# The output gate's units placed behind the last head pair, and the finished rows cut beside that pair's states

## The reference, cut to what matters

```python
def first_block(x, ...):
    h = rmsnorm(x) * (1 + scale) + shift
    p = h @ w_in
    c_val, c_gate, c_og, ts, r_og, g_conv, g_rwkv = split(p)
    u = causal_depthwise_conv(c_val * sigmoid(c_gate), 31 taps)
    u = silu(layernorm(u) * ln_g + ln_b) * silu(c_og)
    y_conv = u @ w_conv_out
    o = rwkv7_scan(token_shift(ts), ...)
    o = groupnorm_and_bonus(o) * silu(r_og)
    y_rwkv = o @ w_rwkv_out
    m = sigmoid(g_conv) * y_conv + sigmoid(g_rwkv) * y_rwkv
    return x + gate * (m @ w_out)
```

## Time and profile before

| | |
|---|---|
| median of 3 runs | 2361.52 us (2360.99 to 2362.99) |
| the profiled execution | 2362.81 us |
| its span in the trace | 2361.5 us, 44695 instructions |
| PE busy | 2215.4 us, 94% of the span |
| DVE, ACT, POOL busy | 1462.9, 938.0, 462.2 us (62, 40, 20%) |
| the scan's periods and all before them | 0 to 680 us |
| last pair's states to the end of stage 5 | 680 to 956 us |
| second block | 956 us to the end |

### The profile page before, as it was taken

How to read it: one execution, slowest core, us unless ns; L and a number is a source line. 1 busy time by engine, 2 the same in 40 slices (tenths; PEclk the granted TensorE clock), 3 DMA queues, 4 the chain that set the end, 5 groups by cost and what they waited for, 6 DMA issues and landing times.

```text
span 2361.5 us, 44695 instructions
## 1 busy us (share of the span) xinstructions
PE 2215.4 (94%) x19538; PEld 1947.2 (82%) x19538; DVE 1462.9 (62%) x2338; ACT 938.0 (40%) x1590; POOL 462.2 (20%) x277
## 2 busy tenths in 40 slices
PE   4898999999997999987998999999999999999999
PEld 1677777777766787976888999999988889999987
DVE  3687888888867443496556666633355556777722
ACT  1324434344332434433544444322456655444411
POOL 0344343344310344423231000000000011000000
PEclk7899999999998999997999999999999999999999
DMA  6541011111115324310013223223311013223231
GB/s 237 128 111 55 11 42 42 42 42 42 42 60 173 107 90 126 118 38 10 21 37 112 90 90 91 91 92 94 109 45 37 21 36 115 90 90 90 86 107 67
DMA packets 60290, 184.75 MB, mean 78 GB/s; under 512 B 7200, under 2 KB 11296, under 8 KB 60096
## 3 DMA queue, kind: packets, MB, share of 16 engines
q1 hardware_dynamic: 60096, 181.90, 24.9%
HBM read 174.99 MB, written 6.88 MB: 77 GB/s over the span
## 4 chain that ended last, share of the span: by engine, by line
PE 74%; DVE 16%; ACT 5%; issue 2%; DMA 1%; POOL 0%; SPq 0%; DVEq 0%; ACTq 0%
PE PS L540 59%; PE PS L670 4%; DVE ca L1874 3%; PE PS L1025 2%; PE PS L1152 1%; PE PS L865 1%; PE PS L1120 1%; DVE Swk L2273 1%; DVE mx L2269 1%; DVE kx L1942 1%; PE PS L998 1%; DVE Bf L1948 1%; DMA xt<-in_xT 1%; ACT Lb L1200 1%; DVE acc L1804 1%
## 5 line engine op out<-in xcount | busy, mean ns | idle before, releaser
L2560 POOL TENSOR_TENSOR wlo<-raw,whi 128x1024 fp32r<-128x1024 f32 (+2 forms) x154 | 310.4, 2017 | 926.5 <-ACT whi L1200 921.1
L540 PE MATMUL PS<-nhi,whi 128*128 128x264 f32 x2064 | 440.1, 294 | 12.5 <-DVE nlo L2115 6.9
L540 PE MATMUL PS<-nlo,whi 128*128 128x264 f32 x2064 | 423.1, 287 | 0.0
L540 PE MATMUL PS<-nhi,wlo 128*128 128x264 f32 x2064 | 420.4, 285 | 0.0
L1200 ACT ACTIVATE whi<-raw 128x1024 fp32r<-128x1024 f32 (+3 forms) x322 | 306.4, 953 | 226.4 <-PE PS L540 199.4
L540 PEld LDWEIGHTS PS<-nhi,whi 128*128 128x128 f32 x2064 | 324.0, 191 | 22.1 <-DVE qB L2157 5.6
L540 PEld LDWEIGHTS PS<-nlo,whi 128*128 128x128 f32 x2064 | 324.6, 190 | 0.0
L540 PEld LDWEIGHTS PS<-nhi,wlo 128*128 128x128 f32 x2064 | 324.0, 191 | 0.0
L1786 DVE TENSOR_TENSOR wlo<-raw,whi 128x1024 fp32r<-128x1024 f32 (+1 forms) x168 | 201.1, 1197 | 171.9 <-ACT whi L1200 171.6
L540 PE MATMUL PS<-hhi,whi 128*128 128x512 f32 x648 | 264.5, 408 | 7.4 <-DVE hlo L1853 7.3
L540 PE MATMUL PS<-hhi,wlo 128*128 128x512 f32 x648 | 258.4, 399 | 1.6 <-POOL wlo L2560 1.6
(11 more groups left out here) (351 smaller groups left out, 3533.8 us busy)
## 6 DMA issues: line engine op xcount, KB each, us to landing
raw<-in_wall SPq DMA_DIRECT2D x282, 512.0 KB, 3.6
raw<-in_wall SPq DMA_DIRECT2D x16, 384.0 KB, 3.1
TZ<-g_rows SPq DMA_DIRECT2D x2, 2112.0 KB, 8.4
raw<-in_wall SPq DMA_DIRECT2D x32, 128.0 KB, 2.0
raw<-in_wall SPq DMA_DIRECT2D x16, 256.0 KB, 2.6
g_rows<-gsb SPq DMA_DIRECT2D x8, 328.0 KB
xt<-in_xT SPq DMA_DIRECT2D x1, 2048.0 KB, 13.8
o_rows<-os SPq DMA_DIRECT2D x8, 256.0 KB, 2.2
```

What stands on the lines that cost most here:

```text
L540: q = e.matmul(out, cuts[a][:, k * P:(k + 1) * P], (hi_, lo_)[b][:, kr, lo:lo + w], start=start and k == 0 and a == b == 0, stop=stop and ...
L2560: e.tensor_tensor(wlo[slot[i]][:, w], raw[i % NRAW][:, w], whi[slot[i]][:, w].bitcast(F32), ALU.subtract).then_inc(*up("lo_pool", i))
```

## The change

What it does, part by part:

- **Last pass.** The ninth pass of `PERIOD` goes; the string `LAST` runs in its place. It has eleven fill units, not three: gate 6, gate 7, rog 7 and the eight units of the output gate c_og (stage 2 is gone from its old place). Between pieces of two f stands one state step of pair 7; the letter y cuts one finished row (ACT `yhi`, DVE `ylo`), k = 0 to 7. Row 7 is cut straight from `os`, without the way through DRAM. The SiLU of c_og unit p waits for the lower part of row p, since both live in `keep8[p]`.
- **Transfers.** SP loads rows 0 to 6 back once the last core step of pair 7 is done (`KV_sum`), before the last pass.
- **rwkv_out.** Its weights' remainder moves from DVE to POOL (`ON_POOL`). The ada units leave this stage. The mean's matmul comes after its sixth unit, into bank 6.
- **g_conv.** The squares of the layer norm run from the seventh rwkv_out unit to the second g_conv unit, the variance's matmul after the third g_conv unit, the normalising and SiLU after it, and the product with `keep8` and the split of its rows beside g_conv units 5 to 7.
- **conv_out.** The ada units stand between its units; their sums live in `t1b`. DVE's two instructions for each now come in the rounds of this stage.
- **out.** The one-column matmuls for `mod` come after its first unit.

```diff
-ON_POOL = ("w_in", "a_in", "out", "a_out", "b_out", "conv_out")
+ON_POOL = ("w_in", "rwkv_out", "a_in", "out", "a_out", "b_out", "conv_out")
...
+LAST = ("fft" + 6 * "sfft" + "sffy" "sfffy" "sfffyt" "sfffy" "fffyffyffy" "s" "fffy" + 35 * "ft")
...
+    if j == 8:
+        return [("gate", 6, 0), ("gate", 7, 0), ("rog", 7, 0)] + [("og", n, 0) for n in range(8)]
...
     for j in range(8):
         units.append(("rwkv_out", j * P, 0, 8))
-        units.append(("ada", 4 + j // 4, j % 4, 8))
-    for base in (2048, 7296):
-        for j in range(8):
-            units.append(("w_in", base + j * P, 0, 8))
+    for j in range(8):
+        units.append(("w_in", 7296 + j * P, 0, 8))
     for j in range(8):
         units.append(("conv_out", j * P, 0, 8))
+        units.append(("ada", 4 + j // 4, j % 4, 8))
...
-        gates = [sb("macc2", z1 + 98304, S), sb("macc3", z1 + 100352, S)]
+        gates = [t1b[:, 0, :], t1b[:, 1, :]]
...
-            for j in range(9):
-                run(PERIOD, ...)
+            for j in range(8):
+                run(PERIOD, ...)
+            run(LAST, s=side(7), f=fill(8), t=nothing(), y=nothing())
...
+                if j == 5:
+                    on.wait_ge(*at("oc", 7))
                     on.wait_ge(*at("conv_sum"))
-                    e.matmul(PS[:, 2, :], ones, acc2[:, :], start=True, stop=True).then_inc(*up("mean_sum"))
+                    e.matmul(PS[:, 6, :], ones, acc2[:, :], start=True, stop=True).then_inc(*up("mean_sum"))
...
                 full("w_in", hhi, hlo, halves(S, b))
+                if j == 2:
+                    on.wait_ge(*at("conv_sq", 7))
+                    e.matmul(PS[:, 7, :], ones, acc1[:, :], start=True, stop=True).then_inc(*up("var_sum"))
...
                 full("out", mhi, mlo, halves(S, b), (lambda k: on.wait_ge(*at("m", k))) if j == 0 else None)
+                for g in (4, 5) if j == 0 else ():
+                    on.wait_ge(*at("ada_dve", ada_unit[g, 3]))
+                    on.wait_ge(*at("mm", 7))
+                    for n in range(4):
+                        q = e.matmul(PS[:, g, n:n + 1], gates[g - 4][:, n * P:(n + 1) * P],
+                                     con[:, CONE:CONE + 1], start=True, stop=True)
...
+                    elif kind == "og":
+                        on.wait_ge(*at("y", p))
+                        act(keep8[:, p, :], src, ACT.Silu).then_inc(*up("og", p))
...
-            on.wait_ge(*at("os", 7))
-            on.wait_ge(s_od, 128)
-            for k in range(8):
-                if k % 4 == 0:
-                    on.wait_ge(s_ol[k // 4], 64)
-                act(yhi[:, k, :], keep8[:, k, :], ACT.Copy).then_inc(*up("y_hi", k))
+            def cut_rows():
+
+                for k in range(8):
+                    if k == 0:
+                        on.wait_ge(*at("Ph", 7))
+                    if k < 7:
+                        on.wait_ge(s_ol[k // 4], (64, 48)[k // 4])
+                    else:
+                        on.wait_ge(*at("os", 7))
+                    act(yhi[:, k, :], keep8[:, k, :] if k < 7 else os_[:, :], ACT.Copy).then_inc(*up("y_hi", k))
+                    yield
...
-                for k in (0, 1, 2) if j == 0 else (j + 2,) if j < 6 else ():
+                for k in {5: (0, 1, 2), 6: (3, 4), 7: (5, 6, 7)}.get(j, ()):
...
-                on.wait_ge(*at("os", j))
-                e.dma_start(odram[j * P:(j + 1) * P, :], os_[:, :]).then_inc(s_od, 16)
-            on.wait_ge(s_od, 128)
-            for k in range(8):
+                if j < 7:
+                    on.wait_ge(*at("os", j))
+                    e.dma_start(odram[j * P:(j + 1) * P, :], os_[:, :]).then_inc(s_od, 16)
+            on.wait_ge(s_od, 112)
+            on.wait_ge(*at("KV_sum", 7))
+            for k in range(7):
                 e.dma_start(keep8[:, k, :], odram[k * P:(k + 1) * P, :]).then_inc(s_ol[k // 4], 16)
```

More of the change, by code:

```diff
@@ L1378, in scalar, with squares @@
             run(BEFORE, c=nothing(), s=nothing(), p=prep(0), f=fill(-1), t=nothing())
-            for j in range(9):
-                run(PERIOD, c=core(j) if j < 8 else nothing(), s=side(j - 1) if j else nothing(),
-                    p=prep(j + 1) if j < 7 else nothing(), f=fill(j), t=nothing())
-            on.wait_ge(*at("os", 7))
-            on.wait_ge(s_od, 128)
-            for k in range(8):
-                if k % 4 == 0:
-                    on.wait_ge(s_ol[k // 4], 64)
-                act(yhi[:, k, :], keep8[:, k, :], ACT.Copy).then_inc(*up("y_hi", k))
+            def cut_rows():
[8 more added lines that the diff above has]
+                    yield
+            for j in range(8):
+                run(PERIOD, c=core(j), s=side(j - 1) if j else nothing(), p=prep(j + 1) if j < 7 else nothing(), f=fill(j),
+                    t=nothing())
+            run(LAST, s=side(7), f=fill(8), t=nothing(), y=cut_rows())
+            def squares(*ks):
+                for k in ks:
+                    on.wait_ge(*at("conv_centred", k))
+                    if k >= 2:
+                        on.wait_ge(*at("conv_sq", k - 2))
+                    act(t1b[:, k % 2, :], uv[:, k, :], ACT.Square).then_inc(*up("conv_square", k))
             for j in range(8):
                 passed()
-            rw_last = [i for i in range(NU) if units[i][0] == "rwkv_out"][-1]
+                if j >= 6:
+                    squares(2 * j - 12, 2 * j - 11)
+            rw_last = count.next - 1
             for j in range(8):
@@ L2042, in vector, with cut_rows @@
             run(BEFORE, c=nothing(), s=nothing(), p=prep(0), f=fill(-1), t=taps(BEFORE.count("t")))
[L2043 to L2059 removed]
+            def cut_rows():
+                for k in range(8):
+                    on.wait_ge(*at("y_hi", k))
+                    e.tensor_tensor(ylo[:, k, :], keep8[:, k, :] if k < 7 else os_[:, :], yhi[:, k, :].bitcast(F32),
+                                    ALU.subtract).then_inc(*up("y", k))
+                    yield
+            for j in range(8):
+                run(PERIOD, c=core(j), s=side(j - 1) if j else nothing(), p=prep(j + 1) if j < 7 else nothing(), f=fill(j),
+                    t=taps(PERIOD.count("t")))
+            run(LAST, s=side(7), f=fill(8), t=taps(LAST.count("t")), y=cut_rows())
             def norm_steps():
@@ L2083, in vector @@
             for j in range(8):
+                i = passed()
+                bg(5)
+                on.wait_ge(*at("unit", i))
+                on.wait_ge(*at("gate_sg", j))
+                e.tensor_tensor(mm[:, j, :], PS[:, 4 + j % 2, :], sg8[:, j, :], ALU.mult).then_inc(*up("mm", j))
+                if j == 3:
+                    for _ in conv:
+                        pass
+                if j >= 3:
+                    next(ns)
+            for j in range(8):
                 passed()
                 next(ns, None)
-            for _ in ns:
-                pass
-            mod_end(4)
-            mod_end(5)
-            for j in range(8):
-                passed()
-                if j == 0:
+                if j == 3:
                     on.wait_ge(*at("conv_rstd"))
@@ L2642, in gpsimd @@
             run(BEFORE, c=nothing(), s=nothing(), p=prep(0), f=fill(-1), t=nothing())
-            for j in range(9):
-                run(PERIOD, c=core(j) if j < 8 else nothing(), s=nothing(),
-                    p=prep(j + 1) if j < 7 else nothing(), f=fill(j), t=nothing())
+            for j in range(8):
+                run(PERIOD, c=core(j), s=nothing(), p=prep(j + 1) if j < 7 else nothing(), f=fill(j), t=nothing())
+            run(LAST, s=nothing(), f=fill(8), t=nothing(), y=nothing())
             while units[count.next][0] != "a_in":
```

92 lines of the change are left out of this document (26 added, 66 removed).

## The result

The changed kernel runs in 2342.89 us (2340.90 to 2345.60), the kernel before, measured with it, in 2361.26 us (2360.67 to 2362.99): ratio 0.9924, 95% interval 0.9912 to 0.9936. Forecast were 2346.0 us, range 2339 to 2353, and faster with 0.93. So the sign and the range held, and the gain is larger than forecast: 18.4 us by the medians, not 15.5.

What follows compares the result with a forecast made beforehand. PE was taken to set the time between 680 and 956 us. Gains of 23.5 us less 8.0 us of cost gave net 15.5: 2362.8 - 15.5 = 2347.3, with runs' median 1.3 lower, 2346.0 us; range 2339 to 2353.

Steps and rivals of the forecast that it cites:

- Long wait and state steps: PE's wait for ylo before rwkv_out goes, gain 17.9 us; pair 7's state steps stop waiting, gain 3.5 us.
- Mean, variance, mod: Mod's one-column matmuls lose the wait between their groups but keep the slow clock behind them; gain 0.5 us.
- out: In the last stage, PE's 1.6 us wait for POOL is covered by mod's 3.6 us; gain 1.6 us.
- POOL in DVE's way: POOL holds DVE instructions with two SBUF inputs, pairs taking 3 to 3.7 us; without this the loss is 3.4, not 8.0.
- Rival A: POOL costs DVE little around conv_out, only 3.4 us lost; gain 20.1 us, time 2341.4 us, chance 0.22.
- Start of conv_out: PE waits 3.5 us for rows and 1.6 us for the second unit's weights; cost 5.1 us.
- Rounds: Conv_out's rounds take 6.25 us with the ada pair on DVE held by POOL; cost 2.9 us.
- Rival B: Conv_out's start: two more row steps held by POOL, and the clock falls; gain 8.7 us, 2352.8 us, chance 0.11.
- C: The long wait before rwkv_out only moves, row 7's lower part coming too late; 2363.9 us, no difference, chance 0.04.
- D: POOL holds product, lower part and pair in every conv_out round, 33.6 us on top; 2379.6 us, slower, chance 0.03.

Runs made afterwards that it cites:

- Rows alone: Changed kernel with the output gate's eight units behind rwkv_out again, rows still cut early; 2354.47 us, ratio 0.9977 to the kernel before.
- Ada interleaved: Changed kernel with each ada unit's two DVE instructions split around the lower part in conv_out's rounds; 2344.42 us, ratio 0.9936 to the kernel before.
- Products first: Changed kernel with all eight products with keep8 issued beside the fifth g_conv unit, before the row-by-row subtractions; 2336.41 us, ratio 0.9900 to the kernel before.
- ada back: Changed kernel with the ada units between the rwkv_out units again, their sums in buffers of their own; 2344.76 us, ratio 0.9934 to the kernel before.
- mod twice: Changed kernel with mod's eight one-column matmuls issued twice over; 2346.91 us, ratio 0.9944 to the kernel before.
- changed, wait in mod: Changed kernel with mod's second matmul group waiting for DVE's step on the first, as before the change; 2343.61 us, ratio 0.9924 to the kernel before.
- remainder on DVE: Changed kernel with rwkv_out's weight remainder made on DVE, not POOL; 2345.68 us, ratio 0.9938 to the kernel before.
- both of these: Changed kernel with all eight products issued first and the ada units split around the lower part; 2339.73 us, ratio 0.9915 to the kernel before.
- before without the wait: Kernel before with mod's second matmul group in its own bank, not waiting for DVE's step on the first; 2360.57 us, ratio 0.9994.

## Why the prediction was right, and where its sizes were off

The stretch gave 17.4 us where the sum said 15.5. Up to V, 22 units now against 19 before, (816.00 - 674.13) - (808.38 - 671.25) + 3×5.60 = 21.5 us were gained; behind V, 4.1 were lost.

- **Long wait and state steps**: forecast 17.9 + 3.5 = 21.4, measured 21.5. This trace runs 2.9 us ahead of before's, on whose clock the forecast stands. Row 7's lower part was forecast for 715 and came at 713.3 + 2.9 = 716.2, rwkv_out for 747.9 and began at 747.8: 32 us to spare, not 33. The taps were done at 753.5, forecast 751, and the mean's first sum, which takes them up, came 17 us later. "Rows alone" shows that the cover of eight units is worth 13.1 us, or 11 without the clock's fall at the start of conv_out, which comes with the cover too.
- **Mean, variance, mod**: the step that failed. I kept 3.6 us ("I keep the slow clock"); `mod` cost 1.84 us, and the clock did not fall. Gain here 2.1 + 2.0 - 1.9 = 2.2 instead of 0.5: nearly the whole error. The earlier trace rows showed one fall in one profile, and I took it for a property of the instructions.
- **out**: I wrote that `mod` covers POOL's 1.6 us fully. A wait of 0.44 us was left, 0.7 with what stands around it, against 1.9 for the 1.6 before: a gain of 1.2, 0.4 less than forecast. The cover was not `mod` alone but also the slow rounds: without them waits of 2.4 us came back.
- **POOL in DVE's way**: forecast 3 to 3.7 us for a pair, measured 3.55; the period 6.25 forecast, 6.19 measured; the earlier trace rows carried it. The Trainium skill's SBUF — State Buffer, "Who interferes with whom", on which this rested, agrees with these rows: two SBUF inputs beside POOL are held (0.69 us becomes 2.11), while `sg<-PS,sg`, with one, takes its own time. Both cases stand side by side in the first round of conv_out after, with a POOL remainder from 844.62 to 846.99 (DVE's timeline):

```profile
845.38 0.69 DVE L2114 TENSOR_TENSOR sg<-PS,sg 128x512 f32<-128x512 f32 x1 [1.06 <-PE PS L543]
846.10 1.43 DVE L2116 TENSOR_TENSOR mm<-mm,sg 128x512 f32<-128x512 f32 x1
```

Rival A, that it costs little, is out. "Ada interleaved" is the test: with the pair out of POOL's way the period is 5.62.
- **Start of conv_out**: first upper part forecast V+17.4, measured V+17.3; the last row V+36.4 against V+35.9; the waits 5.1 us against 4.9. "Products first" removes these four. Three pieces for `ylo` and one for `wlo`, as forecast.
- **Rounds**: 2.9 forecast, 2.6 measured.

Together, the error of 1.9 is 0.1 (long wait) + 1.7 (mod) - 0.4 (out) + 0.5 (start and rounds). By the medians the gain was 18.4, another 1.0 more, which lies outside the stretch. And it is luck that the clock did not fall at the start of conv_out in either profile of the changed kernel (below); such a fall would have taken up to 2.2 us of the gain. The number of rival A (gain 20.1) is near the profiled difference of 20.2, but by 2.9 us of chance ahead of the change. Rival B did not happen in the changed kernel: no further row step was held by a whole POOL instruction, and the clock did not fall at the start of conv_out in its two profiles. But it fell there in five of the seven others that have the waits for `ylo` there (all but "ada back" and "mod twice"), and in none of the three without them, so this part of B was a real risk. "Mod twice" and "changed, wait in mod" are the changed kernel itself up to `out`, so the same instructions gave no fall in three profiles and one in the fourth. Such a fall cost between nothing ("ada interleaved") and 2.2 us ("remainder on DVE"). It does not by itself explain how far the runs of a kernel spread: those of "ada interleaved", with these waits, lie within 2.1 us and those of "both of these", without them, within 4.0; the unedited parts before and behind the stretch alone vary by 3.7 and 3.0 us. The page TensorE: Matmul & The Clock Gate (Part 1) of the Trainium skill has slow as the default that activity releases; these falls, all behind idleness or in and behind one-column work, agree. C did not happen (32 us of slack), nor D: from the second round on POOL held one DVE instruction a round, not three.

## What to carry to other kernels

Move work whose inputs are long ready beside a latency-bound tail, and count what that cover also hides: here the rows were only part, the taps and the clock the rest. Where two engines alternate on a row (product, copy, subtract), issue ahead the half that waits for nobody; one reordered loop gave 4.1 us. And before removing a delay, look one wait further: three edits here (ada interleaved, both of these, before without the wait) saved time that the next wait, for POOL or for the residual, took back.

## What was unexpected of the hardware

- The granted clock falls by chance: with the same instructions and waits at the start of conv_out it was 1.00 in three profiles and 0.50 for 6.8 us in a fourth, and two profiles of one unaltered program differ by 2.7 us behind the stretch (clock 0.86 and 0.91 from 1000 to 1120 us). The scan, unchanged in all kernels, ended anywhere within 3.7 us.
- A wait of 0.29 us on PE costs 0.55 us in all: the matmul behind it comes 0.45 us late, and the next another 0.10.
- Behind 1.84 us of one-column matmuls in full work the clock stayed at 1.00 in all eleven profiles that have them in one block, and in the one with a pause of 0.34 us in the middle; where they were issued twice it fell when they had run for 2.8 us. In the kernel before it fell behind 2.1 us with a pause, right behind the variance's sum; why there, stays open.
